# First down projection as two tile pairs with Strassen steps in the in-place slots; its residual added in place, the strips turned late

## The reference, cut to what matters

```python
# the end of the first block: D_MODEL = 2048, D_FF = 5632
        h = h + mixed @ w_out[l]
        hn = rmsnorm(h, ffn_norm[l])
        h = h + (jax.nn.silu(hn @ w_gate[l]) * (hn @ w_up[l])) @ w_down[l]
    return rmsnorm(h, final_norm)
...
# the start of the second block
        h = rmsnorm_2(x, attn_pre_norm[l])
        proj = h @ w_in[l]
```

## Time and profile before

| | |
|---|---|
| Median of 3 runs | 2487.69 us (2487.3 to 2488.36) |
| The profiled execution | 2488.59 us, span 2487.0 us |
| Mean granted TensorE clock | 0.999 |
| TensorE (PE) busy | 2461.5 us, 99% |
| VectorE (DVE) busy | 1550.5 us, 62% |
| ScalarE (ACT) busy | 1291.0 us, 52% |
| GpSimd (POOL) busy | 46.8 us, 2% |

### The profile page before, as it was taken

How to read it: one execution, slowest core, us unless ns; L and a number is a source line. 1 busy time by engine, 2 the same in 40 slices (tenths; PEclk the granted TensorE clock), 3 DMA queues, 4 the chain that set the end, 5 groups by cost and what they waited for, 6 DMA issues and landing times.

```text
span 2487.0 us, 29920 instructions
## 1 busy us (share of the span) xinstructions
PE 2461.5 (99%) x11325; PEld 2042.9 (82%) x11325; DVE 1550.5 (62%) x1906; ACT 1291.0 (52%) x1611; POOL 46.8 (2%) x96
## 2 busy tenths in 40 slices
PE   9999999999999999999999999999999999999998
PEld 7888888888888888888888778877888888888887
DVE  6455544655788989875445587565565555655444
ACT  6446555445555555554445455564655554544443
POOL 1000100000000000000002000000000000000000
PEclk9999999999999999999999999999999999999999
DMA  7655545555566666655556445555565565565554
GB/s 231 194 176 154 178 152 162 199 188 201 194 198 197 194 203 196 205 192 193 189 193 203 136 152 160 162 186 182 174 194 186 170 200 187 176 194 203 194 190 157
DMA packets 239565, 459.82 MB, mean 185 GB/s; under 512 B 16614, under 2 KB 18832, under 8 KB 239072
## 3 DMA queue, kind: packets, MB, share of 16 engines
q1 hardware_dynamic: 237744, 452.65, 56.1%
q0 software_dynamic: 1680, 5.69, 0.7%
q10 hardware_dynamic: 32, 0.01, 0.0%
HBM read 456.19 MB, written 2.10 MB: 184 GB/s over the span
## 4 chain that ended last, share of the span: by engine, by line
PE 96%; DVE 2%; ACT 1%; issue 1%; DVEq 0%; POOL 0%; ACTq 0%; POOLq 0%
PE acc L615 23%; PE acc L617 23%; PE acc L616 23%; PE acc L916 4%; PE acc L914 4%; PE acc L915 4%; PE acc L634 1%; PE acc L636 1%; PE acc L635 1%; PE mis L916 1%; PE mis L914 1%; PE mis L915 1%; PE mis L588 1%; PE mis L1153 1%; PE mis L713 1%
## 5 line engine op out<-in xcount | busy, mean ns | idle before, releaser
L1755 DVE TENSOR_TENSOR lo<-raw,hi 128x1024 fp32r<-128x1024 f32 (+1 forms) x697 | 842.7, 1221 | 695.5 <-ACT hi L1191 694.0
L1191 ACT ACTIVATE hi<-raw 128x1024 fp32r<-128x1024 f32 (+1 forms) x697 | 724.5, 1055 | 598.5 <-PE acc L617 550.8
L615 PE MATMUL acc<-hi,xb_hi 128*128 128x512 f32 x1248 | 492.7, 395 | 4.3 <-DVE lo L1755 4.3
L617 PE MATMUL acc<-hi,xb_lo 128*128 128x512 f32 x1248 | 486.9, 390 | 0.0
L616 PE MATMUL acc<-lo,xb_hi 128*128 128x512 f32 x1248 | 486.6, 390 | 0.0
L615 PEld LDWEIGHTS acc<-hi,xb_hi 128*128 128x128 f32 x1248 | 234.7, 188 | 57.3 <-DVE lo L1755 9.4
L615 PE MATMUL acc<-hi,xa_hi 128*128 128x512 f32 (+1 forms) x704 | 274.9, 391 | 3.9 <-DVE lo L1755 2.3
L617 PEld LDWEIGHTS acc<-hi,xb_lo 128*128 128x128 f32 x1248 | 234.7, 188 | 49.6
L616 PEld LDWEIGHTS acc<-lo,xb_hi 128*128 128x128 f32 x1248 | 234.7, 188 | 47.4
L617 PE MATMUL acc<-hi,xa_lo 128*128 128x512 f32 (+1 forms) x704 | 271.7, 386 | 0.0
L616 PE MATMUL acc<-lo,xa_hi 128*128 128x512 f32 (+1 forms) x704 | 271.5, 386 | 0.0
(11 more groups left out here) (417 smaller groups left out, 2984.0 us busy)
## 6 DMA issues: line engine op xcount, KB each, us to landing
raw<-in_w_in SPq DMA_DIRECT2D x216, 512.0 KB, 4.0
raw<-in_w_ffn_in SPq DMA_DIRECT2D x176, 512.0 KB, 3.6
raw<-in_w_down SPq DMA_DIRECT2D x88, 512.0 KB, 4.1
raw<-in_w_ffn_out SPq DMA_DIRECT2D x88, 512.0 KB, 4.7
wf_raw<-in_w_gate SPq DMA_DIRECT2D x80, 512.0 KB, 3.5
wf_raw<-in_w_up SPq DMA_DIRECT2D x80, 512.0 KB, 3.7
raw<-in_w_out SPq DMA_DIRECT2D x32, 512.0 KB, 4.3
raw<-in_w_o SPq DMA_DIRECT2D x32, 512.0 KB, 4.3
```

The source lines that it names most:

```text
L615: nc.tensor.matmul(o, xh, wh, start=kb == 0, stop=False)
L617: last = nc.tensor.matmul(o, xl, wh, start=False, stop=kb == k - 1)
L1191: nc.scalar.activation(hi[:, slot, :, 0:width], raw[:, slot, :, 0:width], ACT.Copy)\
L1755: V.tensor_tensor(lo[:, slot, :, 0:width], raw[:, slot, :, 0:width], hi[:, slot, :, 0:width].bitcast(F32), ALU.subtract).then_inc(lo_ready, 1)
```

## The change

**Slots.** The down projection leaves the ring of four and joins the feed-forward in the six in-place slots. It is now two pairs (`d0`: strips 0 and 1, `d1`: strips 2 and 3), each of 22 steps with two chunks. The list `run_b` holds the ten pairs of the feed-forward and these two, and one code serves them all. `places` lays the chunks on the slots and can skip a place in the cycle; it does so in both new pairs, at k = 2 and k = 6. The order of the slots is 1, 0, 3, 5, 2, 4 and was 0, 1, 3, 5, 2, 4.

**Strassen.** Steps k = 4, 7, 10, 13, 16 and 19 (`D_S`) of both new pairs are in Strassen's form. Their weight sums go to one set `td` (the feed-forward has two). The operand forms `ef` are made from the items in `d0` (`ff_forms`: four additions of 128 columns, each waiting for the one before it, and one subtraction more in `ff_split_lo`) and serve `d1` too. `middle`, `middle_end`, `finish` and `finish_up` run at the end of both new pairs as in the feed-forward.

**Residual and strips.** `new_strip` adds a pair's sums to `hres` in place, without a staging buffer. Strips 0 and 1 are turned at the last step of `d1`, strip 2 before chunk 1 of `in2a` and strip 3 before its chunk 3. Their splits (`x2_hi`, `x2_lo`) and the squares (`strip_squares`) of strips 2 and 3 follow in `in2a`. TensorE waits for `finish` of `d1` before it begins `in2a`, and for `finish_up` before its second tile.

In the diff `sp`, `pe`, `act` and `dve` (or `V`) are the engines' queues.

```diff
-F_SLOT = (0, 1, 3, 5, 2, 4)
+D_S = (4, 7, 10, 13, 16, 19)
+PLACES = (1, 0, 3, 5, 2, 4)
...
+        for i in range(DT // 2):
+            run_b.append(Pair(len(run_b), "down", i, KF // CK, D_S, c, g))
+            c, g = c + 2 * KF // CK, g + len(D_S)
...
+        n_ffn, d0, d1 = FT - F_FIRST, run_b[-2], run_b[-1]
+        skips = [d0.chunk(2, 0), d0.chunk(6, 0), d1.chunk(2, 0), d1.chunk(6, 0)]
+        f_slot, f_prev, f_turn = places(F_END, skips)
...
+            for p in run_b:
+                for k in range(p.nk):
                     for h in range(2):
-                        ffn_chunk(i, k, h)
+                        c = p.chunk(k, h)
+                        slot = f_slot[c]
+                        if f_prev[c] is not None:
+                            sp.wait_ge(f_used, f_prev[c] + 1)
...
+            for p in run_b:
                 begun = set()
+                for k in range(p.nk):
...
+                    if p is d0 and k == 2:
+                        pe.wait_ge(ff_out, n_ffn)
+                        turn(i3 - 1, stg, 1)
+                    if p is d0 and k % 2 == 0:
+                        pe.wait_ge(side, i2 + k // 2 + 1)
+                    if p is d1 and k == p.nk - 1:
+                        pe.wait_ge(y_ok, p.no + 1)
+                        for j in range(2):
+                            turn(i3 + j, strip(j), j)
+                    if k in p.forms:
+                        strassen(p, k, begun)
                     else:
...
+            pe.wait_ge(tile_sum, 4 * len(run_b) - 2)
             tile(Count(n0), 0, KD, xb, tiles_of(t0), t0 % 2, sides=i3,
-                 hook={4: lambda: turn(i4 - 1, stg, 0)})
+                 hook={1: lambda: turn(i3 + 2, strip(2), 0), 3: lambda: turn(i3 + 3, strip(3), 1)})
+            pe.wait_ge(tile_sum, 4 * len(run_b))
...
-                act.wait_ge(f_in[f_slot(c)], 16 * (c // 6 + 1))
-                if c < 4:
-                    act.wait_ge(chunk_used, F_OLD - (2 if c >= 2 else RING))
+                act.wait_ge(f_in[f_slot[c]], 16 * f_turn[c])
+                if f_prev[c] is None:
+                    act.wait_ge(chunk_used, F_OLD - (2 if f_slot[c] % 2 else 0))
...
+                first_chunks(after)
+                if after is d0:
                     ff_split_hi(0)
                     ff_split_hi(1)
...
             for c in range(2 * per):
-                if c == LEAD:
-                    keep(i3 + DT - 1, ss_f4, DT - 1)
+                if c < RING:
+                    act.wait_ge(f_used, last_in(2 + (n0 + c) % RING // 2))
+                if c == 2:
+                    x2_hi(0, 0)
+                    x2_hi(1, 1)
+                if c == 3:
+                    x2_hi(2, 0)
+                    strip_squares(2)
+                if c == 4:
+                    x2_hi(3, 1)
+                    strip_squares(3)
+                if c == 6:
                     root(3, rs_f)
...
+            def new_strip(p, h):
+
+                x, j = sums_of(p)[h], 2 * p.i + h
+                dve.wait_ge(tile_sum, 4 * p.no + 2 * h + 2)
+                for t in range(TT):
+                    V.tensor_tensor(hres[:, t, j * W:(j + 1) * W], hres[:, t, j * W:(j + 1) * W], x[:, t, :], ALU.add)\
+                        .then_inc(staged, 1)
...
+                        chain.step(V.tensor_tensor(e, a21, a22, ALU.subtract))
+                        chain.step(V.tensor_tensor(a21, a21, a11, ALU.subtract))
+                        chain.step(V.tensor_tensor(f, a22, a21, ALU.subtract))
+                        V.tensor_tensor(g, a12, f, ALU.subtract).then_inc(ef_sum, 1)
...
             for c in range(2 * per):
-                if c == LEAD:
-                    add(i3 + DT - 1, n, -1, (t0 - 1) % 2, hres[:, :, (DT - 1) * W:])
+                if c == 2:
+                    x2_lo(0, 0)
+                    x2_lo(1, 1)
+                    finish(d1)
+                    new_strip(d1, 0)
+                    finish_up(d1)
+                if c < RING:
+                    dve.wait_ge(f_used, last_in(4 + (n0 + c) % RING // 2))
+                if c == 3:
+                    new_strip(d1, 1)
+                if c == 4:
+                    x2_lo(2, 0)
+                if c == 5:
+                    x2_lo(3, 1)
...
-            pool.wait_ge(chunk_used, PH["in2a"][0])
+            pool.wait_ge(f_used, F_END)
```

More of the change, by code:

```diff
@@ L99, with __init__, chunk, set @@
 F_S = (0, 3, 5)
-F_SLOT = (0, 1, 3, 5, 2, 4)
+D_S = (4, 7, 10, 13, 16, 19)
+PLACES = (1, 0, 3, 5, 2, 4)
 F_FIRST = 1
-F_SKIP = 2
-F_NEW = FT - F_FIRST
-F_PER = 2 * KD // CK
 FD, FE, FF_, FG = 0, 1, 2, 3
+class Pair:
+    def __init__(self, no, stage, i, nk, forms, c0, g0):
+        self.no, self.stage, self.i, self.nk, self.forms, self.c0, self.g0 = no, stage, i, nk, forms, c0, g0
+    def chunk(self, k, h):
+        return self.c0 + 2 * k + h
+    def set(self, k):
+        return self.g0 + self.forms.index(k)
+def places(n, skips):
+    slots, prev, turn, at = [], [], [], 0
+    for c in range(n):
+        at += c in skips
+        slot = PLACES[at % 6]
+        before = [b for b in range(c) if slots[b] == slot]
+        slots.append(slot)
+        prev.append(before[-1] if before else None)
+        turn.append(len(before) + 1)
+        at += 1
+    return slots, prev, turn
 class Count:
@@ new lines, in strassen @@
+            def strassen(p, k, begun):
+                ca, cb, g = p.chunk(k, 0), p.chunk(k, 1), p.set(k)
+                end = k == p.forms[-1]
+                late = "c11" not in begun
+                sa, sb = f_slot[ca], f_slot[cb]
+                b11, b21 = ([wf[:, sa, j, kk, :] for j in range(2)] for kk in range(2))
+                t3, b22 = ([wf[:, sb, j, kk, :] for j in range(2)] for kk in range(2))
+                tt = t_set(p, k)[0]
+                t1, t2, t4 = ([tt[:, j, f, :] for j in range(2)] for f in range(3))
+                form = forms(p, k)
+                a11, a12, a22 = operand(p, 2 * k, 0), operand(p, 2 * k + 1, 0), operand(p, 2 * k + 1, 1)
@@ L979, in plain_pair @@
                     for kk in range(CK):
[L980 removed]
+                        w2 = [wf[:, f_slot[c], j, kk, :] for j in range(2)]
                         for t in range(TT):
[L982 removed]
+                            last = product(outs[t], operand(p, 2 * k + kk, t), *w2, touch(p, names[t], begun),
+                                           end and kk == 1)
@@ new lines, in strip_squares, with x2_hi @@
+            def strip_squares(j):
+                act.wait_ge(staged, stages(i3 + j))
+                act.wait_ge(squares, SQ["h"] + j)
+                for t in range(TT):
+                    last = square(hres[:, t, j * W:(j + 1) * W], stg2[:, t, :], ss_f4[:, 4 * t + j:4 * t + j + 1])
+                last.then_inc(squares, 1)
+            def x2_hi(j, pair):
+                side_hi(i3 + j, xb, 4 * j, [gfin[:, 4 * j + q:4 * j + q + 1] for q in range(4)], pair=pair)
+            i3 = PH["down"][2]
```

527 lines of the change are left out of this document (274 added, 253 removed).

## The result

The changed kernel takes 2493.17 us (median of 10 runs, 2492.55 to 2495.1), the kernel before 2487.59 (10 runs, 2487.19 to 2488.69). The ratio is 1.0024, 95% interval 1.0014 to 1.0033: slower by 5.6 us, and forecast was +4.3 with a range of 2487.5 to 2497. Its profiled execution has a span of 2491.5 us, 4.4 above that of before.

A forecast was written before the change was run, and what follows sets the result against it. TensorE, busy 99% of the span, bounds the kernel. -8.2 + 1.2 + 1.4 + 0.2 + 3.6 + 2.6 = +0.8, plus 3.4 for the clock: +4.2, median 2492 us; own range 2490.5 to 2494, 8-in-10 range 2487.5 to 2497.

The forecast's parts named there:

- Saving, -8.2: Two down pairs, six Strassen steps each: 36 matmuls fewer at 0.227 us, -8.2 us.
- Entry of the feed-forward, +1.2: Feed-forward start: ScalarE's copy of the second chunk waits for the old tile, so TensorE waits, +1.2 us.
- Seam to down, +1.4 and +0.2: Down projection's entry: TensorE waits for the last pair's sums, +1.4; at k = 4 for a turned item's copy, +0.2 us.
- Inside the pairs, 0: Inside d0 and d1: VectorE (14.6 of 15.6 us in the first pair) and the ring keep up, no wait, 0 us.
- VectorE or the ring falls behind: Rival, in the pairs: TensorE waits in steps and at (7,1), +3 more, 2495 to 2496 us; chance 0.12.
- the 0.5 that the forecast named as a sign of being wrong: In the pairs: waits of more than 0.5 at k = 4, 7, ... would show the forecast wrong.
- the bound of 0.9: In each pair: if the load of (7,1) lands after 5 us, some 0.9 us is lost, as upper bound.
- Seam to in2a, +6.2: Down to in2a: wait for d1's sums before the first chunk, +3.6, and before the fifth, chunk 4, +2.6 us.
- the seam is covered after all: Rival, at in2a's entry: the 6.2 and their clock vanish, -5.4, 2482.3 us, faster; chance 0.08.
- The clock, +3.4: Behind the new long waits TensorE's clock falls twice, 1.7 us each, +3.4; bounds none and three (5.1).
- Sum: All terms before the clock give +0.8 us; with the clock +4.2 on the profiled execution's 2488.59, median 2492 us.
- the forecast took off 0.9: The profiled execution before, 2488.59 us, lies 0.9 over its runs' median of 2487.69, so the forecast median is 2492.

The follow-up runs named there:

- Three steps less: Changed kernel with three Strassen steps in each down pair (k = 4, 10, 16) and not six, 18 matmuls more: 2497.03 us.
- The fifth chunk: Changed kernel with ScalarE splitting in2a's fifth chunk ahead of strip 3's high halves and squares: 2488.81 us.
- the sums first: Changed kernel with VectorE doing d1's sums (finish) ahead of the low halves of strips 0 and 1 at in2a's entry: 2490.66 us.
- the run that missed the gap: Kernel with all seams mended, plus ScalarE making a second-projection chunk's high half ahead of the gate's exponential; the gap stayed 2.40: 2478.41 us.
- two medians of single-seam runs: Changed kernel with both queues reordered at in2a's entry, 2487.84 us; changed kernel with in2a's fifth chunk split ahead of strip 3's halves and squares, 2488.81 us.

## Why the prediction was right

**Saving, -8.2.** Right. From the first matmul of the down projection to the start of its last are 235.53 us, 1.5 of them lost to the low clock, against 242.87 before. That is 8.8 less. One turn less (0.8) and 0.2 of small gaps stand in it, which leaves 8.2. Three steps less cost 3.9 of 4.1.

**Entry of the feed-forward, +1.2.** Measured 1.3 (a gap of 1.55 in place of 0.23), and it went when ScalarE's wait went.

**Seam to down, +1.4 and +0.2.** Measured 1.6: the sums stood where the walk through the queue had them, behind two items and two chunks (the wait ended at 1082.27, the walk had 1080.45 plus the 1.3 of the entry, which is 0.5 early). At k = 4 of `d0` two matmuls start 0.34 and 0.31 after the one before, 0.2 together beyond the pitch. This trace has no wait there by name; that of "The fifth chunk", where the first of the two is 0.61, names the one that was forecast, ScalarE's copy of the turned item:

```profile
PE mis L953 <- ACT ff_raw L1526: 0.2, 1, 0.2
```

**Inside the pairs, 0.** Right for the profiled execution, and with as little to spare as forecast: VectorE's 39.7 of 42 us make 14.7 of 15.6, where the forecast had 14.6. The rival "VectorE or the ring falls behind" would have been true at every other step, and a little of it is true in some executions. Two experiments whose code in the pairs is the same show one wait each at k = 4 of `d1`, where the ring's distance is five behind the skipped place: 0.4 with the sums first, 0.6 in the run that missed the gap, which is more than the 0.5 that the forecast named as a sign of being wrong. In the latter the four loads ahead of it landed as the first line says (us from issue to landing, least, median, most; the same four of the changed kernel in the second):

```profile
DMA to landing us min/median/max: 3.9/5.3/7.0
```

```profile
DMA to landing us min/median/max: 3.8/4.0/4.9
```

So the bound of 0.9 stood for something real, but it was put at the wrong chunk. The load of chunk (7,1), on which the forecast built it, took 3.4 to 3.8 us in both pairs of all twelve traces that have the skips. The late one is that of chunk (4,1) in `d1`, which is issued 0.4 us behind another. It took 4.8 to 6.1 us in nine of these traces, the changed kernel's 4.9 among them, and no gap followed; it took 6.4, 6.8 and 7.0 in three, and TensorE's starts were 0.35, 0.74 and 1.02 apart there. Why it lands so late in some executions is open.

**Seam to in2a, +6.2.** Measured 3.79 - 0.23 = 3.6 and 2.83 - 0.23 = 2.6, each as forecast, and each removed by turning the rows of the queues that the forecast named. The forecast's own chain for the second gives a little less than it says (13.4 + 5.15 is 18.55 and not 18.7, so 2.45), and the measured 2.6 is nearer to what it wrote than to what it added. The rival "the seam is covered after all" falls.

**The clock, +3.4.** Right in size, and partly by luck. The forecast had two falls of 1.7 each. In the profiled execution two of the three new gaps were followed by a fall. The one behind 3.05 cost about 1.5; the one behind 3.79 cost about 3, since it lasted for a whole chunk and half a turn. Against them the old fall behind 2.4 didn't come, which saves 1.3 to 1.6: from that gap to the next one near 1505 us the trace of before takes 101.6 us and this one 100.3. Together that is about +3. So the second fall was priced 1.3 too low, and a fall that stayed out, which wasn't in the sum, took about as much away. What was called unsure there, whether a condition lies near these lengths, is now measured: 14 of 27 gaps between 2.4 and 3.1 us were followed by a fall, and all six of 3.8 and more. Of the clock's rise, when steady work begins, the Trainium skill (TensorE: Matmul & The Clock Gate, "What you observe") says that its moment varies from run to run; here it is the fall that comes in some executions and not in others, behind the same gap of 2.4. That is also the likely reason why two medians of single-seam runs lie 1.8 below what their gaps give: each of their traces has one fall where that of the unedited change has two. What decides whether the clock falls behind one of these gaps, the runs don't show.

**Sum.** The gaps of the profile and the saving give +1.1 (forecast +0.8), its clock about +3, and small pieces the rest of 4.4. The median lies 1.2 over the forecast, within its own range of 2490.5 to 2494. Most of that is one step: the forecast took off 0.9 because the profiled execution of before lay so far over its median, and the changed kernel's (2493.18) lies on its median.

## What to carry to other kernels

When a stage moves into shared buffers, walk both queues row by row across its two seams: here the pairs themselves gave what their matmuls promised, and all of it was lost in rows that stood too far back. A final sum that frees an accumulator goes ahead of any work that isn't wanted before the next chunk. Count gaps of TensorE of 2.4 us and more from start to start twice: once for their length and once for what the clock may take, 1.3 to 3 us here, in some executions; a spread between runs of that size can be its sign.

## What had not been expected of the hardware

- The length of a gap alone doesn't tell whether the clock falls behind it: it did 14 times in 27 from 2.38 to 3.06 us, never in 40 at 1.3 to 1.96, always in 6 at 3.8 and more. Removing one such gap leaves the others as they were: with the sums first, the clock fell behind the gaps of 2.80 and 2.39, behind which it had stayed up in the unedited change.
- A fall behind 3.8 us lasted for 12 starts, all but the first 0.43 apart, in four of five traces (8 in the other), one behind 2.4 us for 7 or 8.
- At the lower level a start comes every 0.43 us, for which the Trainium skill (TensorE: Matmul & The Clock Gate, "Wait — 56ns, not 53.3ns?") has 426.7 ns; the trace agrees. At the upper level the same section of the Trainium skill has 215.7 ns, and here it is 0.227 us in undisturbed chunks (12 starts in 2.72 us); for this kernel the measurement decides.
